# Reordering the second block of a two-block transformer kernel: Gelu, tile borders and the end of the mixer

## The reference

```python
for l in range(2):                                   # second_block
    h = _rmsnorm(x, pre_mix_norm[l])
    h = _hybrid_mixer_2(h, ...)                      # below
    x = x + _rmsnorm(h, post_mix_norm[l])
    h = _rmsnorm(x, pre_ffn_norm[l])
    u = _causal_dwconv(h @ ffn_up, ffn_conv) + ffn_conv_bias   # 3 taps, 2 x 2816 columns
    gate, val = jnp.split(u, 2, axis=-1)
    h = (gelu(gate) * val) @ ffn_down
    x = x + _rmsnorm(h, post_ffn_norm[l])

def _hybrid_mixer_2(h, ...):
    a_qkv, a_z, a_b, a_a, b_q, b_k, b_v = split(h @ w_in)
    aq, ak, av = split(silu(_causal_dwconv(a_qkv, dn_conv)))   # 4 taps
    o_a = gated_delta_rule(l2norm(aq), l2norm(ak), av, g(a_a), sigmoid(a_b))
    o_a = _rmsnorm(o_a, dn_out_norm) * silu(a_z)
    o_b = dilated_attention(rope(b_q), rope(b_k), b_v)
    return concat([o_a, o_b]) @ w_out
```

## Time and profile before

| | us |
|---|---|
| median of 3 runs (2065.55 to 2076.42) | 2065.92 |
| the profiled execution's own time | 2066.17 |
| its span, first to last instruction | 2064.3 |
| PE busy | 1919.4 (93%) |
| DVE busy | 1223.1 (59%) |
| ACT busy | 996.8 (48%) |
| POOL busy | 652.8 (32%) |

### The profile page before, as it was taken

One profiled execution on the slowest core, in us unless ns is written; L12 is line 12 of the kernel. 1 busy time (PEld: TensorE's weight loads), 2 busy tenths in 40 slices (PEclk: granted clock), 3 DMA queues, 4 the chain that ended last, 5 costly groups with the idle time before them and its releaser, 6 DMA issues.

```text
span 2064.3 us, 41181 instructions
## 1 busy us (share of the span) xinstructions
PE 1919.4 (93%) x15758; PEld 1870.1 (91%) x15758; DVE 1223.1 (59%) x1478; ACT 996.8 (48%) x1304; POOL 652.8 (32%) x595
## 2 busy tenths in 40 slices
PE   6999999999999999999999989879999889779997
PEld 6999999999989999999999989769889789679897
DVE  4655586666456456866664674446664664356655
ACT  5434456544444345564444563445544564445543
POOL 4751301276137513012662016122330025032220
PEclk9999999999999999999999899989999799889999
DMA  6646444465455464444555422114445222124444
GB/s 221 209 164 210 154 144 145 162 206 193 164 195 201 157 215 164 144 146 159 206 190 168 154 102 100 42 64 144 175 144 199 90 102 87 37 82 163 166 164 159
DMA packets 49222, 314.39 MB, mean 152 GB/s; under 512 B 5713, under 2 KB 6865, under 8 KB 19921
## 3 DMA queue, kind: packets, MB, share of 16 engines
q1 hardware_dynamic: 48960, 311.09, 43.7%
q10 hardware_dynamic: 144, 1.69, 0.2%
HBM read 311.71 MB, written 1.05 MB: 152 GB/s over the span
## 4 chain that ended last, share of the span: by engine, by line
PE 62%; DVE 10%; issue 9%; ACT 9%; DMA 5%; POOL 2%; ACTq 1%; DVEq 0%; SPq 0%; POOLq 0%
PE ps L541 15%; PE ps L543 15%; PE ps L542 15%; DMA raw<-in_down_dram 4%; ACT w_hi L1109 4%; DVE w_lo L1567 4%; PE ps L858 3%; PE ps L546 3%; PE ps L547 3%; PE ps L548 3%; DVE conv L1886 2%; ACT conv L1160 2%; PE ps L691 1%; PE ps L731 1%; DVE v L2084 1%
## 5 line engine op out<-in xcount | busy, mean ns | idle before, releaser
L1567 DVE TENSOR_TENSOR w_lo<-raw,w_hi 128x2048 fp32r<-128x2048 f32 (+1 forms) x322 | 713.0, 2215 | 423.6 <-ACT w_hi L1109 423.1
L541 PE MATMUL ps<-xn,w_hi 128*128 128x256 f32 x2688 | 768.5, 286 | 59.6 <-DVE w_lo L1567 14.6
L542 PE MATMUL ps<-xn,w_hi 128*128 128x256 f32 x2688 | 755.7, 281 | 0.0
L543 PE MATMUL ps<-xn,w_lo 128*128 128x256 f32 x2688 | 755.5, 281 | 0.0
L1109 ACT ACTIVATE w_hi<-raw 128x2048 fp32r<-128x2048 f32 (+1 forms) x322 | 562.4, 1748 | 126.5 <-DMA raw<-in_down_dram 83.4
L541 PEld LDWEIGHTS ps<-xn,w_hi 128*128 128x128 f32 x2688 | 516.9, 192 | 74.2 <-issue 44.1
L542 PEld LDWEIGHTS ps<-xn,w_hi 128*128 128x128 f32 x2688 | 515.4, 192 | 0.8 <-issue 0.5
L543 PEld LDWEIGHTS ps<-xn,w_lo 128*128 128x128 f32 x2688 | 515.1, 192 | 0.0
L541 PE MATMUL ps<-h,w_hi 128*128 128x256 f32 x1056 | 294.1, 278 | 4.9 <-DVE w_lo L1567 4.8
L542 PE MATMUL ps<-h,w_hi 128*128 128x256 f32 x1056 | 293.2, 278 | 0.0
L543 PE MATMUL ps<-h,w_lo 128*128 128x256 f32 x1056 | 293.2, 278 | 0.0
(11 more groups left out here) (310 smaller groups left out, 2633.2 us busy)
## 6 DMA issues: line engine op xcount, KB each, us to landing
raw<-in_gu_dram SPq DMA_DIRECT2D x132, 1024.0 KB, 4.9
raw<-in_in_dram SPq DMA_DIRECT2D x70, 1024.0 KB, 4.9
raw<-in_down_dram SPq DMA_DIRECT2D x96, 704.0 KB, 4.1
raw<-in_out_dram SPq DMA_DIRECT2D x16, 1024.0 KB, 4.8
raw<-in_pb_dram SPq DMA_DIRECT2D x4, 1024.0 KB, 4.8
raw<-in_pa_dram SPq DMA_DIRECT2D x4, 1024.0 KB, 4.9
tables_all<-in_tables_dram ACTq DMA_DIRECT2D x1, 1648.0 KB, 7.2
rows<-in_rows_dram SPq DMA_DIRECT2D x2, 768.0 KB, 5.5
```

Of the source, the lines that this page charges most:

```text
L541: pe.matmul(out, w, xh, start=first, stop=False)
L542: pe.matmul(out, w, xl, start=False, stop=False)
L543: return pe.matmul(out, wl, xh, start=False, stop=last)
L1567: dve.tensor_tensor(w_lo[:, r, 0:elems], raw[:, k % RAW_RING, 0:elems], w_hi[:, r, 0:elems], ALU.subtract).then_inc(lo.sem, 1)
```

## The change

Parts of the code move, mostly in the second block:

1. **Gelu.** In the up projection's rounds ACT now does: both `conv<-ps` of tile pair j, the split of slot j + 3, and then the Gelu of pair j. `rounds` gets an argument `behind` for it, and its order is otherwise body, then split, with the first split (`open_rounds`) set ahead of the root of the norm.
2. **Borders.** For down projections the splits run one slot further ahead of the body (`tile_rounds`). In the first block's out stage the low part of x is made one chunk later than before.
3. **Down and out, from PSUM.** ACT squares each tile straight from PSUM, and copies it to `hm` times the gain; DVE's copies are gone. PE adds each square by a matmul of ones behind the next tile (`chunk_square`); POOL's seven additions are gone. The `out` stage uses six PSUM banks.
4. **x.** `post` is now two operations a chunk without the gain; DVE does chunks 0, 2, 3, 5, 6 and POOL chunks 1, 4, 7, both operations. Between the blocks POOL scales x in two operations of 2048 elements, in place of DVE's eight.
5. **Mixer, first part.** The small product for decay and beta moves from behind slot 1 to behind slot 0, its weights are cut earlier; `query_column` and `turn_k` move into slot 5, `decay_rows_of(1)` behind it; `turn_v` behind side slot 1; DVE's `scaled` steps follow.
6. **Mixer, end.** Unit 0's transposes and unit 1's scores move half a slot earlier; the scores of units 2 and 3 are computed and masked ahead of the delta rule's chain, in other PSUM banks; the output's norm is done in two halves; `out` starts with the four attention chunks of its first three slots, and takes the delta rule's chunks after.
7. **Start.** ACT's queue issues x and the small inputs, so that SP starts with the weights. The first slot is split ahead of x; ACT and POOL each square half of x in one operation.
8. **End.** The last layer loads and splits no slots for a layer that doesn't come.

```diff
-            def gate_gelu(j, g):
+            def gate_taps(j, g):
                 ...
                 taps(at, st, j, 1, up_w[:, layer, i + FC, 2:3], up_b[:, layer, bass.ds(i + FC, 1)], g)
+
+            def gelu(j, g):
                 act.wait_ge(conv_ok.sem, conv_ok.upto(at, 36 + 3 * j + 3 + 12 * g))
                 act.activation(silu_gate[:, j % 2], conv[:, j % 2, 0], ACT.Gelu_apprx_tanh).then_inc(gate_ok.sem, 1)
-            rounds(act, at, st2["gu"], SLOT_DOWN, FC, 1, split, gate_gelu)
+            open_rounds(at, st2["gu"], split)
+            rounds(act, at, st2["gu"], SLOT_DOWN, FC, split, gate_taps, gelu)
...
+    def rounds(eng, at, st, nxt, count, split, body, behind=None):
         def step(j, g):
             body(j, g)
+            split(at, st.slot0 + j + 1 + LEAD, g, st.elems)
+            if behind:
+                behind(j, g)
...
+    def tile_rounds(eng, at, st, nxt, split, body, steps=cycle):
+        def step(j, g):
+            split(at, st.slot0 + 2 * j + 1 + LEAD, g, st.elems)
+            split(at, st.slot0 + 2 * j + 2 + LEAD, g, st.elems)
+            body(j, g)
...
+        def square_out(at, gain, c, src, sq):
+            act.activation(sq[:, c], src, ACT.Square).then_inc(squared.sem, 1)
+            act.activation(hm[:, c], src, ACT.Copy, scale=gains2[:, 4 * at[1] + gain, c:c + 1]).then_inc(x_new.sem, 1)
...
+        def chunk_square(at, n, c, src):
+            pe.wait_ge(squared.sem, squared.upto(at, KC * n + c + 1))
+            ins = pe.matmul(ps[:, AUX, 0:T], ones_d[:], src[:, c], start=c == 0, stop=c == KC - 1)
...
+            pe.wait_ge(yb_lo.sem, yb_lo.upto(at, 2))
+            out_part(0, 0, WC)
+            out_part(1, 0, WC)
+            out_part(2, 0, WC)
+            pe.wait_ge(o_rooted.sem, o_rooted.upto(at, 2))
+            for j in range(3):
+                out_part(j, WC, KC)
+                if j:
+                    chunk_square(at, 0, 2 * j - 2, sq_out)
+                    chunk_square(at, 0, 2 * j - 1, sq_out)
+            out_part(3, 0, KC)
...
-                for c in range(KC):
-                    dve.scalar_tensor_tensor(v[:, c], hm[:, c], gains2[:, 4 * layer + k, c:c + 1], rstd[:, 0:T],
-                                             ALU.mult, ALU.mult).then_inc(post_v.sem, 1)
+                for i, c in enumerate(DVE_ADDS):
+                    dve.tensor_tensor(v[:, c], hm[:, c], rstd[:, 0:T], ALU.mult).then_inc(post_dve.sem, 1)
...
+        def add_post(at, k):
+            for i, c in enumerate(POOL_ADDS):
+                pool.tensor_tensor(v[:, c], hm[:, c], rstd[:, 0:T], ALU.mult).then_inc(post_pool.sem, 1)
+                pool.tensor_tensor(x[:, c], x[:, c], v[:, c], ALU.add).then_inc(x_pool.sem, 1)
```

More of the change, by code:

```diff
@@ L525, in _ @@
             stream(at, st2["down"], io["down3"])
-        for k in range(LEAD):
-            load((2, DEPTH), k, 0, SLOT, io["in2"][0, k])
         for c in range(KC):
@@ L651, in tile @@
                     last.then_inc(used.sem, 1)
+                    if behind_tile and j and not half:
+                        behind_tile(j - 1)
+            if behind_tile:
+                for j in range(st.pairs):
+                    tile(j, 0)
+                behind_tile(st.pairs - 1)
+                return
             tile(0, 0)
@@ L734, in attend_pv, with short_scores, short_turn, short_pv @@
             last.then_inc(pv.sem, 1)
+        def short_scores(at, u):
+            pe.wait_ge(projected.sem, projected.upto(at, 8))
+            score(at, u, q_t, lambda lane, hd, kl: k_t[lane, hd // 2, 0:kl], scores, 2 * (u - 2))
+        def short_turn(at, u):
+            pe.wait_ge(masked.sem, masked.upto(at, 6))
+            pe.wait_ge(probs.sem, probs.upto(at, GROUP * (u + 1)))
+            for k in range(GROUP):
+                last = pe.transpose(ps[:, u - 2, k * P:(k + 1) * P], soft[:, 0, k, (u - 2) * P:(u - 1) * P], ident[:])
+            last.then_inc(p_turned.sem, 1)
+        def short_pv(at, u, v_at):
+            g = UNITS[u][1]
+            pe.wait_ge(masked.sem, masked.upto(at, 8))
+            pe.wait_ge(p_out.sem, p_out.upto(at, TURNS[u]))
+            for hh in range(GROUP):
+                k = GROUP // 2 * (hh % 2) + hh // 2
+                last = pe.matmul(ps[:, u, hh * HD:(hh + 1) * HD], p_t[:, u - 2, k],
+                                 v_at[:, 0, (GROUP * g + hh) * HD:(GROUP * g + hh + 1) * HD], start=True, stop=True)
+            last.then_inc(pv.sem, 1)
         def attend_out(at, t, bank=AUX):
@@ L1437, in _ @@
                 roots_of_two_norms(at)
-            copy(ba_hi[:], ba_raw[:, layer]).then_inc(ba_split.sem, 1)
             act.activation(warm[:, 1:2], eps[:, 0:1], ACT.Silu)
@@ L2057, in _ @@
[L2057 to L2067 removed]
+            attend_norm(at, 2, 1)
@@ L2094, in _ @@
+                add(len(DVE_ADDS) - 1)
+                if k == 3 and layer < DEPTH - 1:
+                    for c in range(3, KC):
+                        scale_next(c)
             post(1)
```

500 lines of the change are left out of this document (295 added, 205 removed).

## The result

The changed kernel takes 2013.58 us in the median of four runs (2012.45 to 2021.05); the kernel before took 2065.74 beside it. The ratio is 0.974, 95% interval 0.971 to 0.978: a gain of 52 us where the prediction had 78. 2013.6 us lies outside the predicted range, which ended at 2009.

What follows compares the result with a forecast made beforehand. PE bounds the first block; the second block's up projection is bound by an ACT-DVE loop, and `out` waits for POOL. Terms 26 + 25 + 0 + 2 + 15 + 4 + 6 = 78 us gave 1988 us, range 1966 to 2009.

Steps and rivals of the forecast that it cites:

- Gelu: Second block's up projections: with slot j + 3 split ahead of the Gelu, PE becomes the bound; 26 us less.
- the prediction's own two prices: Up projections, 32 rounds: gain of 25.9 us at PE's faster matmul pace, 19.2 at the slower.
- Mixer's end: Mixer up to `out`: earlier scores and norm start `out` sooner; net 12.5 us a layer, 25 in all.
- a rival: More than forecast: fewer pauses keep the clock at 2.4 GHz through the mixer, 18 us more, 1970 us; chance 0.12.
- First part of the mixer: Mixer's first part, both layers: waits go as things are asked for later or made earlier; 15 us, bounds 5 and 20.
- Ends of down: Down projections' ends: seven chunk sums between tiles instead of eight behind; 1 us each, 2 in all.
- Start: Kernel start: slot 0 split ahead of x, x landing perhaps 1 us later; 4 us less, between 1 and 5.
- Waits of the borders: Stage borders: waits for `w_lo` in down stages and for `hv` behind a root shrink; 6 of 7.7 us.
- Update of x: `post` behind `out`: DVE 10 operations, POOL 6, 6.3 us for 6.8, but no gain counted.
- Port: Rival: DVE and POOL block each other fully in `post`, 8.5 us; 7 us later in all, 1995 us; chance 0.04.
- Pace: Rival: PE's two matmul paces fall anew; two more slow stretches in the first block cost 14 us, 2002 us; chance 0.13.
- the rivals with a smaller gain: Slow matmul stretches 2002 us (0.13), mixer end as long 1999 (0.10), Gelu half hidden 1998 (0.08), full port block 1995 (0.04).

Runs made afterwards that it cites:

- run 2: Changed kernel with the columns of rstd turned right behind slot 1, ahead of the small product, as before; 2009.34 us, ratio 0.972.
- run 3: Changed kernel with the first block's last norm applied to x by eight DVE operations instead of two on POOL; 2018.75 us, ratio 0.977.
- run 9: Two mixes of restored parts on the changed kernel, both with a late last split: sums behind, 1997.47 us; sums between tiles and three mixer moves undone, 2006.08 us.
- run 8: Changed kernel with three parts as before: rstd columns ahead of the small product, block 1's last norm on DVE, the whole start; 2005.82 us, ratio 0.968.
- run 11: Changed kernel with rstd columns first, last norm on DVE, x by SP ahead of slot 0, sums behind, seven update columns on DVE; 1998.54 us, ratio 0.965.
- run 6: Changed kernel with the eight chunk sums of the second block's down projections behind the last tile again; 2015.92 us, ratio 0.975.
- run 10: Changed kernel with seven of eight columns' updates of x on DVE and one on POOL, instead of three on POOL; 2015.68 us, ratio 0.973.
- run 7: Changed kernel with POOL's two 2048-element operations on x cut into 16 of 256 elements; 2016.14 us, ratio 0.974.
- run 1: The changed kernel measured again with no edit; 2016.24 us, ratio 0.975.

## Why the prediction was wrong

The direction and the two large terms were right, the sum was not: by the profiles 32.6 us are missing of 77.8, and 19.1 of them in one term. Step by step:

- **Gelu, right.** 22.1 us for 26; one of two layers ran at the slow pace, and by the prediction's own two prices that makes (26 + 19) / 2 = 22.5. It was a fault to take the faster pace for both when nothing chose it.
- **Mixer's end, right and larger**: 34.8 for 30.2, `out` at 1337.81 for the forecast 1338.7, although the stages ahead gained nothing. The granted clock rose from 0.84 to 1.00 with the pauses gone, which I had put into a rival.
- **First part of the mixer, wrong: the step that failed.** "Each is for something now asked for a tile later or made earlier" gave 15 us with bounds 5 and 20; it came to -4.1. Three causes, each with its run: the turn of rstd's columns went behind 48 matmuls, with a split behind its copy on DVE (run 2: 7.9 us); POOL's two long operations, which I had counted at "nothing either way", held DVE (run 3: 5.8 us); and where both are mended, PE waits for `q` and `gam` in the place of `rhs_w` (run 9), so that the three moves give some 3 to 5 us in both layers together. With the first two mended, the gain over the kernel before is 5.1 to 7.4 us (runs 8, 9, 11), half of the forecast at most.
- **Ends of down, wrong**: 2 forecast, -7.3 measured, with the down projections themselves. I set seven sums between tiles against eight behind and left out that each waits for ACT's square (3.6 us in five waits), and that in layer 0 the splits ahead of root and reciprocal cover the eight (run 6, where 5.7 us come back; the rest is open).
- **Start, wrong**: "x lands perhaps 1 us later" held for x (0.2 us), but everything waits for the small inputs too, and the last of them came 4.5 us later; and the order put x's work behind slot 0. +4 forecast; the first matmul came 3.5 us later, less the 2.3 us wait that did go: -1.2.
- **Waits of the borders, short**: 6 of 7.7 us forecast. The waits for `w_lo` went from 4.8 to 2.3, those for `hv` from 2.9 to 3.1 in three instead of one: 2.3 us.
- **Update of x**: 0 forecast, and `out` with it -4.0 for -5.4. That the total came near is luck: `out` itself grew by 0.8 us a layer and not by the sums' 2.7, while the granted clock over it rose from 0.90 to 1.00, and the pause behind, counted at nothing, grew by 1.2. The price of sharing was about right: 0.46 us lost for each POOL operation was 0.52, DVE's ten operations took 6.5 us (from 1367.60 to the split at 1374.12) for the 6.3 forecast, and by the rival *Port* it would have been 8.5. What the forecast did not ask is what the part is worth without POOL (run 10). The Trainium skill's rule (page "SBUF — State Buffer", section "Who interferes with whom"), that such instructions of the two engines block each other for the whole instruction, fits the order of events: run 7 shows the hold instruction by instruction.
- **Pace, right as a mechanism**: it took 4.6 us of the Gelu's gain in the one slow layer, and one more slow network in block 1 is 7.0 us by the estimate above. Whether that is why block 1 gave 3.7 for 10 is open: start and borders alone lack 8.9 there and in the down projections, and run 1 ended block 1 at the same time with a slow network less. Pace was a rival of its own, as an alternative. It is a spread on every forecast, and belonged on top of each.

Why the range missed: the rivals with a smaller gain were taken one at a time, and three terms (first part, ends, start) lay outside their own bounds, because I bounded them by the waits seen before and not by what the new order puts in front of them.

What stays open: what picks the pace of a network; and why block 1 differs by some 5 us between executions beyond it (runs 1, 9 and 11), where the traces show more or less time at the lower granted clock but not why.

## What to carry to other kernels

When an instruction is moved, read what stands behind it on its own engine and on the engine that reads its result: a small product moved ahead of a two-column turn held a split of 2.3 us. A wait taken away is worth what is next in line, and in a stage with six waits of 1 to 3 us that is most of it. Before giving DVE's work to GpSimd, time the pair: here the two together were slower than DVE alone. When a start waits for several inputs, look at the landing of each: 1 KB held up everything here.

## What the hardware showed

- Matmuls of 256 columns with fp32r operands start 0.1132 or 0.1176 us apart, both at a granted clock of 1.00 (1414 and 1361 in 160 us). Which it is falls mostly by network and anew in each execution of the same program (1350 and 1406 in one stretch, run 1). Block 1's four networks alone could make 28 us of it (an estimate, 4 x 7.0).
- DVE's short operations in SBUF start 0.34 us apart alone and 0.86 beside POOL's; a 2048-element split takes 2.29 us alone, 2.81 beside POOL operations of 256 elements, 6.67 beside one of 4.59 us. The ones that read PSUM kept their time (`conv_in`, two in 0.74 beside POOL's in run 7 and in 0.75 us alone in run 3).
- Small transfers asked for while weight slots of 1 MB are under way land with the slots: 64 KB and 1 KB took 9.4 and 9.3 us on ACT's queue, and 4.2 and 4.6 to 4.8 on SP's ahead of the slots. x, 1 MB and asked for first, took 5.0 and 4.7 to 4.8.
